# A two-layer transformer kernel on one core: how routed tokens are picked, the order of woven products, a third modulation tile, and small transposes for the last head pair

## The reference

```python
h = rmsnorm(x, norm1_g); proj = h @ w_in            # one product feeds three branches
y_rwkv = rwkv7_branch(u_rwkv, ...) @ w_rwkv_out     # 8 heads of 64, a scan over tokens, both directions
y_attn = dilated_attention_branch(u_attn, ...) @ w_attn_out
x = x + (gates[0] * y_rwkv + gates[1] * y_attn) @ w_out
moe = hier_moe(rmsnorm(x, norm2_g), ...)            # 32 experts, 2 for each token
x = x + moe
# second block, DEPTH_2 = 2 layers, each conditioned on a vector c:
mod = silu(c) @ w_ada[l] + b_ada[l]                 # 1024 x 6144, split into six vectors of 1024
h = rms_norm(x, g_mix) * (1 + sc_m) + sh_m          # then two attentions, a merge, a gated FFN
```

## Time and profile before

| | |
|---|---|
| median of three executions | 2790.33 us (2789.9 to 2797.85) |
| the profiled execution, its own time | 2795.81 us |
| its span, first to last instruction | 2794.0 us |
| mean granted TensorE clock | 0.991 |
| busy: PE, DVE, ACT, POOL | 96%, 56%, 34%, 5% of the span |

### The profile page before, as it was taken

One profiled execution on the slowest core, in us unless ns is written; L12 is line 12 of the kernel. 1 busy time (PEld: TensorE's weight loads), 2 busy tenths in 40 slices (PEclk: granted clock), 3 DMA queues, 4 the chain that ended last, 5 costly groups with the idle time before them and its releaser, 6 DMA issues.

```text
span 2794.0 us, 45154 instructions
## 1 busy us (share of the span) xinstructions
PE 2686.6 (96%) x19214; PEld 1978.5 (71%) x19214; DVE 1570.4 (56%) x2952; ACT 945.8 (34%) x1643; POOL 139.3 (5%) x237
## 2 busy tenths in 40 slices
PE   8999999999999989999999999999999999999999
PEld 6877777877543333357777778888877777788887
DVE  5666676756433323356785566665556865633443
ACT  6243334345201000033455442223324455332221
POOL 0010100110000000000000000010000000000000
PEclk9999999999999999999999999999999999999999
DMA  5233333364599999953352336663232532233332
GB/s 166 77 111 118 92 112 112 94 243 167 216 402 427 426 426 427 426 211 92 98 113 103 127 108 190 192 198 126 72 109 84 121 114 99 83 98 98 98 98 76
DMA packets 149984, 471.64 MB, mean 169 GB/s; under 512 B 14640, under 2 KB 41888, under 8 KB 137232
## 3 DMA queue, kind: packets, MB, share of 16 engines
q1 hardware_dynamic: 114720, 367.62, 36.7%
q0 software_dynamic: 24976, 82.71, 9.5%
q10 hardware_dynamic: 10080, 18.35, 2.2%
HBM read 451.05 MB, written 21.51 MB: 169 GB/s over the span
## 4 chain that ended last, share of the span: by engine, by line
PE 80%; DMA 8%; DVE 6%; ACT 3%; issue 2%; ACTq 0%; SPq 0%; POOL 0%; DVEq 0%
PE psum L154 77%; PE psum L157 4%; DMA wslot<-in_w_gate 3%; DMA wslot<-in_w_up 3%; DVE halfL L163 1%; DMA m_in<-in_w_ada 1%; ACT halfH L160 1%; ACT slot L160 1%; DVE X L163 0%; DVE slot L163 0%; DVE vb L163 0%; DVE gx L163 0%; DVE m_acc L169 0%; ACT L160 0%; DMA X<-in_x 0%
## 5 line engine op out<-in xcount | busy, mean ns | idle before, releaser
L163 DVE TENSOR_TENSOR halfL<-ring,halfH 128x1024 fp32r<-128x1024 f32 x302 | 368.0, 1221 | 529.8 <-ACT halfH L160 529.3
L160 ACT ACTIVATE halfH<-ring 128x1024 fp32r<-128x1024 f32 x302 | 317.4, 1054 | 701.7 <-PE psum L154 699.7
L154 PE MATMUL psum<-hH,halfH 128*128 128x512 f32 x1200 | 482.6, 402 | 1.7 <-DVE hL L169 1.7
L154 PE MATMUL psum<-hH,halfL 128*128 128x512 f32 x1200 | 469.7, 391 | 0.0
L154 PE MATMUL psum<-hL,halfH 128*128 128x512 f32 x1200 | 469.4, 391 | 0.0
L154 PEld LDWEIGHTS psum<-hH,halfH 128*128 128x128 f32 x1200 | 226.0, 188 | 73.8 <-issue 23.5
L154 PEld LDWEIGHTS psum<-hH,halfL 128*128 128x128 f32 x1200 | 226.2, 188 | 48.4
L154 PEld LDWEIGHTS psum<-hL,halfH 128*128 128x128 f32 x1200 | 226.3, 189 | 43.3
L154 PE MATMUL psum<-wslot,XT 128*64 128x512 f32 x1024 | 236.3, 604 | 17.9 <-DMA wslot<-in_w_gate 15.1
L154 PE MATMUL psum<-halfH,hH 128*128 128x512 f32 (+2 forms) x576 | 217.9, 378 | 2.8 <-ACT U L160 1.3
L154 PE MATMUL psum<-halfH,hL 128*128 128x512 f32 (+2 forms) x576 | 208.6, 362 | 0.0
(11 more groups left out here) (498 smaller groups left out, 4098.5 us busy)
## 6 DMA issues: line engine op xcount, KB each, us to landing
wslot<-in_w_gate SPq DMA_DIRECT2D x32, 2048.0 KB, 25.2
wslot<-in_w_down SPq DMA_DIRECT2D x32, 2048.0 KB, 25.7
ring<-in_w_in SPq DMA_DIRECT2D x120, 512.0 KB, 3.7
wslot<-in_w_up SPq DMA_DIRECT2D x30, 2048.0 KB, 26.5
ring<-in_w_gu SPq DMA_DIRECT2D x88, 512.0 KB, 3.6
m_in<-in_w_ada POOLq DMA_DIRECT2D x96, 256.0 KB, 3.2
m_in<-in_w_ada POOLq DMA_DIRECT2D x48, 512.0 KB, 4.8
ring<-in_w_down SPq DMA_DIRECT2D x44, 512.0 KB, 3.3
```

What stands on the lines that cost most here:

```text
L154: return self.e.matmul(*a, **k)
L160: return self.e.activation(*a, **k)
L163: return self.e.tensor_tensor(*a, **k)
```

## The change

Five edits in four parts.
1. The tokens are picked with `xn2` read as it lies, 512 values in a row; half 0 now holds features 0 to 511. ACT sorts at eviction: it reads PSUM with a step of eight and writes runs of 64. Both halves are needed for every k, so all eight transposes now stand behind `slots(0)` and a wait for the second eviction.
2. In the recurrence, `more()` stands ahead of `block`.
3. The first layer's modulation has three input tiles instead of two. The room comes from `m_turn0`: the eighth tile of a group is overwritten by the transposed sum, and counts as used only after the reduction.
4. For the last pair, `rw_turned` uses 16 products of 64x64 (`turned`) instead of four transposes, and ACT copies the result in one instruction instead of four.

```diff
-    m_in0, m_acc0, m_turn0 = [rk(f"m_in0{i}", 512) for i in range(2)], rk("m_acc0", 512), rk("m_turn0", 512)
+    m_in0, m_acc0, m_turn0 = [rk(f"m_in0{i}", 512) for i in range(3)], rk("m_acc0", 512), None
...
-    picked = [sb(f"picked{n}", EX_AT + 4096 + 1024 * n + 128, 512) for n in range(2)]
+    picked = sb("picked", EX_AT + 4096 + 128, 2, 1024)[:, :, 0:512]
...
+                if (i - 4) * 19 // 24 > (i - 5) * 19 // 24:
+                    yield from more()
                 if pr and 5 <= i < 11:
                     yield "block", pr, (i - 5) % 2, TURNS[(i - 5) // 2][0]
-                if (i - 4) * 19 // 24 > (i - 5) * 19 // 24:
-                    yield from more()
...
-            turned_by_two(bank(b), US[:, pr, :]).then_inc(*up("rw_pe", "y_turned", pr))
+            (turned_by_two if pr < 3 else turned)(bank(b), US[:, pr, :]).then_inc(*up("rw_pe", "y_turned", pr))
...
-                    x = xn2[:, tb, :].rearrange("q (p k) -> q k p", k=8)[:, 4 * half:4 * half + 4, :]
-                    i = pe.matmul(bank(b), Sel32[:, tb, :], x, start=tb == 0, stop=tb == 3)
-                    if (half, tb) == (1, 1):
-                        first_turned(0)
+                    i = pe.matmul(bank(b), Sel32[:, tb, :], xn2[:, tb, 512 * half:512 * half + 512], start=tb == 0,
+                                  stop=tb == 3)
                 i.then_inc(*up("moe_pe", "picked", half))
                 free[b] = [("picked_out", half)]
             slots(0)
-            first_turned(1)
+            pe.wait_ge(*at("picked_out", 1))
+            for half in range(2):
+                b = 6 + half
+                clear(b)
+                for n in range(4):
+                    i = pe.transpose(bank(b)[:, n * 128:(n + 1) * 128], picked[:, half, n * 128:(n + 1) * 128], ident)
+                i.then_inc(*up("moe_pe", "xt", 0, half))
+                free[b] = [("XT", 0, half)]
...
-                ac.activation(picked[half], bank(4 + half), COPY).then_inc(*up("moe_act", "picked_out", half))
+                ac.activation(picked.rearrange("s n (k p) -> s n k p", k=4)[:, :, :, 64 * half:64 * half + 64],
+                              bank(4 + half).rearrange("s (p n k) -> s n k p", n=2, k=4),
+                              COPY).then_inc(*up("moe_act", "picked_out", half))
...
-            sorted_out(US[:, 4 + pr, :], bank(y_bank(pr))).then_inc(*up("rw_act", "yT", pr))
+            if pr < 3:
+                i = sorted_out(US[:, 4 + pr, :], bank(y_bank(pr)))
+            else:
+                i = ac.activation(US[:, 4 + pr, :], bank(y_bank(pr)), COPY)
+            i.then_inc(*up("rw_act", "yT", pr))
...
-                                            op1=AD).then_inc(*up(D, "m_used", L, n))
+                                            op1=AD).then_inc(*up(D, *(("m_used", L, n) if k < 7 or L else ())))
                 if k == 7:
+                    to = m_turn if L else m_in[n % len(m_in)]
                     ve.wait_ge(*now(D))
-                    ve.transpose(m_turn, acc).then_inc(*up(D))
+                    ve.transpose(to, acc).then_inc(*up(D))
...
+                    if L == 0:
+                        also(D, "m_used", L, n)
...
-            if n >= 2:
-                po.wait_ge(*at("m_used", L, n - 2))
+            u = len(m_in)
+            if n >= u:
+                po.wait_ge(*at("m_used", L, n - u))
```

More of the change, by code:

```diff
@@ L2344, in modulation @@
                 if k == 0:
-                    ve.tensor_scalar(acc, m_in[n % 2], cact[:, 0:1], None, M).then_inc(*up(D, "m_used", L, n))
+                    ve.tensor_scalar(acc, m_in[n % len(m_in)], cact[:, 0:1], None, M).then_inc(*up(D, "m_used", L, n))
                 else:
-                    ve.scalar_tensor_tensor(out=acc, in0=m_in[n % 2], scalar=cact[:, k:k + 1], in1=acc, op0=M,
-                                            op1=AD).then_inc(*up(D, "m_used", L, n))
+                    ve.scalar_tensor_tensor(out=acc, in0=m_in[n % len(m_in)], scalar=cact[:, k:k + 1], in1=acc, op0=M,
+                                            op1=AD).then_inc(*up(D, *(("m_used", L, n) if k < 7 or L else ())))
                 if k == 7:
+                    to = m_turn if L else m_in[n % len(m_in)]
                     ve.wait_ge(*now(D))
-                    ve.transpose(m_turn, acc).then_inc(*up(D))
+                    ve.transpose(to, acc).then_inc(*up(D))
                     ve.wait_ge(*now(D))
                     ve.tensor_reduce(m_sum.rearrange("p c x -> p (c x)")[:, b * g:b * g + b],
-                                     m_turn.rearrange("p (b r) -> p b r", r=32), AX,
+                                     to.rearrange("p (b r) -> p b r", r=32), AX,
                                      AD).then_inc(*up(D, *(("m_sum", L) if b * (g + 1) == 192 else ())))
+                    if L == 0:
+                        also(D, "m_used", L, n)
                 yield
@@ L3239, in modulation @@
             g, k = n // 8, n % 8
-            if n >= 2:
-                po.wait_ge(*at("m_used", L, n - 2))
-            po.dma_start(m_in[n % 2], T["w_ada_2"][L, k * 128:(k + 1) * 128,
-                                                   g * w:(g + 1) * w]).then_inc(*landed(f"m_in{n % 2}", "m_in", L, n))
+            u = len(m_in)
+            if n >= u:
+                po.wait_ge(*at("m_used", L, n - u))
+            po.dma_start(m_in[n % u], T["w_ada_2"][L, k * 128:(k + 1) * 128,
+                                                   g * w:(g + 1) * w]).then_inc(*landed(f"m_in{n % u}", "m_in", L, n))
         for n in range(96):
```

## The result

The changed kernel takes 2772.62 us (median of 4, 2770.93 to 2774.61) against 2790.11 (median of 4, 2788.03 to 2797.85): ratio 0.9934, 95% interval 0.9921 to 0.9947, 17.5 us faster. The forecast was 2776, 14.4 us faster. A second set of five gave 2772.85 and 0.9941 (0.9928 to 0.9955).

What follows compares the result with a forecast made beforehand. It took TensorE's chain, busy 80% of the span, as the bound, the experts' weights second. Gains of 5.4 + 4.0 + 4.7 + 0.3 = 14.4 us gave 2776 us on the median's scale, range 2767 to 2788.

Steps and rivals of the forecast that it cites:

- The likeliest case: Whole kernel: the gains of all four parts add to 14.4 us, giving 2776 us; chance 0.56.
- Part 1, 5.4 us: Routing: picks read in one piece and an eviction still 0.60 us start the first expert 5.4 us earlier; bounds 0.2 to 6.9.
- The clock as it was: Picking: the low clock lasts as in the profiled trace, so 4.9 picks take 0.85 us and 11.1 take 0.43.
- Part 2, 4.0 us: Recurrence, pairs 1 to 3: the slice covers TensorE's wait for ACT at step 6, 3 x 1.5 us, 4.0 taken.
- bound 0: Recurrence, lower bound for the reordered slice: TensorE's wait only moves to DVE and nothing is gained; upper bound 6 us.
- Part 3, 4.7 us: First layer's modulation: a third tile cuts DVE's waits; three quarters of TensorE's 6.3 us waiting for DVE gained; bounds 1 to 10.
- Part 4, 0.3 us: Last pair's turn: ACT's copying 0.9 us less, TensorE's products 0.6 more, 0.3 gained; bounds -1.0 and +0.6.
- The clock: Rival, routing: low clock at the first expert costs 2 us, at the picks too all 5.4; 2778 to 2781; chance 0.06.
- Slower: Rival, recurrence: a block's sort on ACT waits behind a copy to DRAM, up to 3.72 us each; 2806 with eight; chance 0.04.
- Only the picking: Rival: the recurrence's waits only move, TensorE waiting for DVE's next eviction instead; 2785 us; chance 0.13.
- only the recurrence: Rival: weights set the experts' start, so nothing of the picking's gain is left; 2781 us; chance 0.08.
- Signs: Trace checks: no step 6 wait, tile waits under 5 us, eviction near 0.60, TensorE idle 90 to 600 us down about 8.

Runs made afterwards that it cites:

- the repeat of each: The kernel before run again unchanged, giving its second trace: 2792.14 us; the changed kernel run again unchanged: 2772.85 us.
- part 2 alone: The kernel before with only the woven slice put ahead of the block, on all engines: 2783.81 us, ratio 0.9974.
- TensorE's order alone: The kernel before with the woven slice ahead of the block on TensorE only, ACT and DVE keeping the old order: 2791.45 us, ratio 1.0004.
- beside part 2: The kernel before with both the woven slice ahead of the block and the third modulation tile: 2778.21 us, ratio 0.9961.
- warming: The changed kernel with 15 more small identity products on TensorE ahead of the picking, run twice: 2772.55 and 2769.82 us.
- the single parts: Four kernels, each the kernel before with one of the four parts, in order: 2783.18, 2783.81, 2785.25 and 2787.41 us.
- the misplaced fill: The changed kernel with small identity products in four places; those in pair 1's loop ran after the wait, not in it: 2770.46 us.

## Why the prediction was right

The likeliest case came true, a little larger. By its own steps:

- **Part 1, 5.4 us.** The traces give 16.67 - 12.29 = 4.4 and, with the repeat of each, 17.23 - 11.05 = 6.2. The picks take 0.43, or 0.85 at the low clock, the sorted eviction 0.597 as the plain one did, so the rule on PSUM patterns (the Trainium skill, "SBUF — State Buffer", Door 1: The DMA port swizzle), which speaks of matmuls, does not carry over to ACT here. "The clock as it was" was the loose assumption: it was low for six of the ten us of picks in one trace, less in the other. The expert began 12.29 and 11.05 us after the first pick, 11 being forecast, and 9.35 where the clock stayed up. DMA's pause shrank as said, and the gain lasted.
- **Part 2, 4.0 us.** 5.7. The mechanism was right: the split no longer stands behind a sort, and DVE goes on earlier. The term was too small, for one reason: the prediction counted TensorE's three waits of 1.5 and took DVE's earlier start only as the reason that they are not lost, while that start is worth something beyond them (in pair 1's steps TensorE's waits for DVE slots were 1.7 us before and are 0.4 with part 2 alone, beside 1.6 and 0.2 for ACT). And its bound 0, "the wait only moves to DVE", is what the kernel with TensorE's order alone does.
- **Part 3, 4.7 us.** 4.7 alone, 5.1 beside part 2 (10.8 - 5.7). Waits left: 2.2 us. That it met its number is in part luck: three quarters of 6.3 was a guess, and the second trace of before has 3.9 in place of the 6.3.
- **Part 4, 0.3 us.** 0.3 by its rows.
- **The sum.** 14.4 forecast; by the rows 10.8 + 0.3 and 4.4 to 6.2 for the picking, 15.5 to 17.3. The mis-sized term is part 2. The interval of the median difference, 14.8 to 22.0 us around 17.5, holds these sums; the forecast's 14.4 lies just below it.
- **The rivals.** The clock took some of part 1 (1.7 to 2.9 us, what warming gives back), at the picks and not, as supposed, at the eight transposes behind them (the clock reads 0.99 to 1.00 from 728 to 740 us). A stretch at half clock in the expert stage, 774 to 782 us before, is still there at 751 to 759. "Slower", by a sort behind a copy that waits for its staging tile, did not happen: of such waits for copies of the woven projection there is one after, 2.8 us at 261.90 and thus behind the last sort of its pair (255.77), where there was one of 3.7 before. "Only the picking" and "only the recurrence" are excluded by the single parts.
- **Signs.** TensorE's wait at step 6 is 0.24, DVE's waits 2.2 (under 5 was said), the eviction 0.60. TensorE's idle time from 90 to 600 us fell by 9.3 us, from 23.7 to 14.4, where about 8 was said. The spans differ by 23.0 and not by 14.4, since before had lost 3.4 us to the clock in the recurrence against 1.7, another 3.4 between 597 and 635 us against none, and 2.07 before its `lora` (109.19 against 107.12); at the picks it was the other way round.

## What to carry to other kernels

A wait in a list names the engine that came last, not the job that made it late. Move a step in every engine's order, and read where each queue's next job then stands: here TensorE's reordering alone was worth nothing, and with ACT's it was worth 5.7 us. Before believing a sum of single parts, give every trace the same correction (time lost at the low clock, counted from a common row) and have a second trace of the unchanged kernel. Better still, find a stretch that repeats to hundredths from trace to trace and read the edit's worth there. Fill a wait that lies ahead of dense products with harmless ones, but only into a bank that is free before the wait ends.

## What the runs showed of the hardware

- An f32 product of 512 columns whose moving operand is read with a step of eight values takes 0.92 us, read in one piece 0.43, or 0.85 at 1.2 GHz; with the step, the low clock (granted 0.50) made it no longer.
- ACT reads PSUM with a step of eight values, and writes SBUF in runs of 64, in 0.597 us, as in one piece.
- Falls of the granted clock often came right behind waits of TensorE: after 2.21 and 1.39 us at the routing, after 2.23 and 0.91 in pair 1's loop, after 2.33 at the turn of `qa`. With products in the wait it did not fall at the routing in three of three traces. The wait of some 1.2 us in pair 0's loop was followed by a fall in one trace of before (0.61 in 212 to 216 us) and not in the other, and with the misplaced fill a wait of 2.23 was followed by none.
- Whatever precedes it, the time from first expert to the next norm is 471.6 to 474.5 us, and an earlier start is passed on whole. DMA runs full there, at 425 to 428 GB/s from 800 us on, and TensorE's longest waits are for weight tiles (15.1 us for those of `w_gate` before, 12.1 after); that the weights set the pace is the likely reading, and no run took them away.
